# Hybrid attention block with 16384 experts on one core: gate products in two fp32r passes, second rows by ScalarE, choice stage of 19 expert groups

## The chip, the cores and the metric

One Trainium2 chip, of which the kernel uses one core. The metric is the device time of one execution in microseconds (us); lower is better.

## What is computed

One layer on 512 tokens of width 2048, float32. First attention of 16 heads with a projection in and out, then an expert layer: each of 8 heads chooses 16 of 16384 experts per token by two halves of 128 keys each (product keys), and the tokens' outputs are the chosen experts' values, weighted.

```python
def peer_ffn(xn, w_pq, sub_keys, u, v):
    ...
    s = jnp.einsum('thcd,hcnd->thcn', q, sub_keys, preferred_element_type=jnp.float32)
    s1, i1 = lax.top_k(s[:, :, 0], PEER_TOPK)
    s2, i2 = lax.top_k(s[:, :, 1], PEER_TOPK)
    ...
    top_s, pos = lax.top_k(cand, PEER_TOPK)
    idx = jnp.take_along_axis(cidx, pos, axis=-1)
    g = jax.nn.softmax(top_s, axis=-1).astype(xn.dtype)
    ...
        ub = u[ib]
        h = jax.nn.gelu(jnp.einsum('ted,td->te', ub, xb), approximate=False)
        vb = v[ib]
        return jnp.einsum('te,ted->td', gb * h, vb)
```

## The kernel before

It is written engine by engine: each engine's queue is a list in the order of the code, and semaphores tie the lists together. PE is TensorE (matmuls), DVE is VectorE, ACT is ScalarE, POOL is GpSimd, SP is SyncE with the queue that issues most DMAs.

Weights stream through in units of 1 MB. For each unit `load` (SyncE) brings it to `raw`, `split_hi` (ScalarE, L399) writes its high half `wh` in fp32r, `lo` (VectorE, L1128) the rest `wl`, and PE multiplies three times (high by high, high by low, low by high; L419 to L421 in `gemm`, L444 to L446 in `chunk_unit`). Two buffers of each: the hi of unit k+1 waits for PE's end of unit k-1.

The expert layer is dense for 336 of the 512 tokens: for all 128 blocks of 128 experts it computes gelu of tokens times `u`, multiplies by a table of gates (zero for what was not chosen), and multiplies by `v`. Another 128 tokens, and a strip of 48 (32 and 16, the "pair" rows) for `u` alone, are done by gathers of single rows: a "dot" (L1494 for the strip, L1596) multiplies a gathered row of `u`, and L1617 adds a gathered row of `v`.

The experts are in 32 groups of 4 blocks. The first `LAG` = 17 groups have their `u` units in the **choice stage** (68 units, counted k = 0 to 67, each one gemm of 16 x 3 matmuls of 336 columns), in which VectorE also finishes the choice and the gates are built. Then 15 **main groups** of 4 `u` and 4 `v` units each, then the **tail**: the `v` units of the 17 groups, two groups to a set of 8 units.

The gates are built in 96 batches of 4 tokens, two batches to a unit, from unit `GATE_FROM` = 16 to 63. For a token, 128 slots (head, rank) are on the partitions. The product of two 128x128 matrices, one holding a one at the slot's second key (`gh`, by L1456), the other holding the slot's weight at its first key (`hot_gate`, by L1469), gives the token's table of gates. Before, this is an fp32 matmul (L1970); on PE it stands inside the unit's gemm, behind the 6th and the 12th of 16 steps. ScalarE copies it out two batches at a time, one unit later (L1063), and every 8 batches a piece of 2 MB goes to `gate_scratch`; the next piece's first copy waits for that store.

The order on VectorE in unit k: lo(k+1), rows of the first batch of unit k+1 (`hot(ahead)`), a lookup or a pair dot where the tables `LOOK_AT` and `DOT_UNITS` say so, rows of the second batch. On ScalarE: gelu of unit k-1 (L1029), hi(k+1), the two copies, and in every second unit the weight rows of the next unit's first batch in VectorE's place (`rows_act`, L1038 and L1043). These wait only for the gate product that frees the buffer:

```python
                act.wait_ge(minus_done, b // 32 + 1)
                act.wait_ge(gate_done, b + 1)
```

`lookup` (L1433 to L1440) turns a rank into a key index by three operations; `take_slots` copies the turned slots of 128 tokens; `turn_pair` (PE) and `take_pair` replace the weights of the 48 tokens once their dots are done. After the stage SyncE issues, in this order, the acts and the gates of group 0 (L668, L672) and the weights of the second main unit; VectorE's `gate_mult` (L1584) waits for the former ahead of its lo for the latter.

Of the kernel before, what the change touches and what calls it, by code (L numbers as in the profile page):

```python
# [35 lines left out]
P = 128  # L36
# [14 lines left out]
LAG = 17  # L51
# [10 lines left out]
GATE_FROM = 16  # L62
# [4 lines left out]
LOOK_AT = {1: GATE_FROM, 3: GATE_FROM + 38}  # L67
# [5 lines left out]
ACT_ROWS = [_b for _b in range(0, (TD - PT - PB) // 4, 2 * GATE_STEP)]  # L73
# [3 lines left out]
DOT_UNITS = sorted([8, 9, 11, 12, 13, 14, 15] + list(range(20, 39)) + list(range(21, 38, 3)) +  # L77
                   list(range(40, 52)) + list(range(42, 52, 3)))
assert len(DOT_UNITS) == PN + NB and DOT_UNITS[PN - 1] == 38 and DOT_UNITS[PN] == 40
assert GATE_FROM == 16 and UT % 16 == 0 and FULL == UT // GT and PAIR_TURN < GATE_FROM + (SLOTS - PB - PT) // 4 + 32  # L80
# [59 lines left out]
def build(nc, x, attn_g, w_f, w_in, b_forget, q_g, k_g, w_out, ffn_g, ffn_row, w_pq, sub_keys, u, v, u_rows,  # L140
          v_rows, out):
    ctx = ExitStack()
    with ctx:
# [99 lines left out]
        look = gl[:, 0:1024]  # L243

        minus_g = at(7040, P)
        gate_piece = at(0, NKEYS * GT)
        h_out = [at(9616 + D, UT), at(9616 + D + UT, UT)]
        hot_gate = [at(8592, 512), at(8592 + 512, 512)]
# [90 lines left out]
        minus_done = sem("minus_done")  # L339
        diff_step = sem("diff_step")  # L340
# [483 lines left out]
        def _(act):  # L824
# [206 lines left out]
            def rows_act(b):  # L1031

                mine = slotT[b // 32 % 2]
                act.wait_ge(minus_done, b // 32 + 1)
                act.wait_ge(gate_done, b + 1)
                for n in range(4 * (b % 32), 4 * (b % 32) + 4):
                    dst = hot_gate[b % 2][:, n % 4 * P:n % 4 * P + P]
                    nc.scalar.activation(dst, iota128[:], ACT.Abs, bias=mine[:, 0, n:n + 1],  # L1038
                                         scale=-1.0).then_inc(diff_step, 1)
                for n in range(4 * (b % 32), 4 * (b % 32) + 4):  # L1040
                    dst = hot_gate[b % 2][:, n % 4 * P:n % 4 * P + P]
                    act.wait_ge(diff_step, 4 * ACT_ROWS.index(b) + n % 4 + 1)
                    last = nc.scalar.activation(dst, dst, ACT.Relu, bias=mine[:, 2, n:n + 1],  # L1043
                                                scale=minus_g[:, n:n + 1])
                last.then_inc(row_done, 1)

            for k in range(N_PROUNITS):
# [75 lines left out]
        def _(dve):  # L1123
# [327 lines left out]
            def hot(b):  # L1451
# [635 lines left out]
```

## Time and profile before

| | us |
|---|---|
| median of 3 runs | 3251.55 (3249.18 to 3255.22) |
| the profiled execution | 3252.24 |
| its span in the trace | 3250.5 |
| PE busy | 3216.1 |
| VectorE busy | 2263.4 |
| ScalarE busy | 1119.1 |
| GpSimd busy | 933.6 |

The trace begins at the first instruction; what lies around the span is 1.7 us. Matmuls are pipelined: a matmul's recorded length is longer than its slot, so the cost of one is read from start to start. The same holds in a lesser degree on VectorE and ScalarE, where an instruction begins before the recorded end of the one before.

### The profile page before, as it was taken

To read this page: it belongs to the slowest core of one execution; us is meant where nothing else is said; L and a number is where in the kernel's file an instruction comes from. 1 tells how busy PE (TensorE), PEld (TensorE's weight loads), DVE (VectorE), ACT (ScalarE), POOL (GpSimd) and SP (SyncE) were. 2 spreads that over 40 slices of the span, in tenths; PEclk is the share of its full clock that TensorE was granted. 3 is DMA by queue.
4 is the path that set the end of the run, shared out by engine and by line. 5 is a ranking of instruction groups with operands and counts; after the bars stand their busy time and mean duration, and the time that the engine had idled before them with its cause. 6 is when DMAs were issued, how large, how long until landed. Compare 5 with 4: busy or idle time off the path is not lost. (4 is left out here: it accounts for less than half of the span.)

```text
span 3250.5 us, 41510 instructions
## 1 busy us (share of the span) xinstructions
PE 3216.1 (99%) x16730; PEld 2818.6 (87%) x16730; DVE 2263.4 (70%) x2636; ACT 1119.1 (34%) x1172; POOL 933.6 (29%) x424
## 2 busy tenths in 40 slices
PE   8999999999999999999999999999999999999999
PEld 6878778887878899999999899889989988888887
DVE  5666541113027888887874888888889888888887
ACT  5232323334232233655553223223222322222221
POOL 4333333333434321111101323223322321223222
PEclk9999999999999999999999999999999999999999
DMA  3222222223233247889877989999989998888888
GB/s 144 78 78 90 77 78 78 78 78 141 92 116 121 88 161 255 304 316 318 311 243 265 352 333 352 336 341 345 358 332 335 350 343 312 320 336 340 343 319 317
DMA packets 171364, 777.87 MB, mean 239 GB/s; under 512 B 14064, under 2 KB 80752, under 8 KB 86384
## 3 DMA queue, kind: packets, MB, share of 16 engines
q1 hardware_dynamic: 127488, 457.77, 38.6%
q0 software_dynamic: 43776, 318.79, 26.3%
q8 instruction: 60, 0.98, 0.1%
q14 instruction: 40, 0.33, 0.0%
HBM read 731.10 MB, written 44.34 MB: 239 GB/s over the span
## 5 line engine op out<-in xcount | busy, mean ns | idle before, releaser
L419 PE MATMUL bank<-xh,wh 128*128 128x336 f32 (+1 forms) x3184 | 1105.8, 347 | 1.6 <-DVE wl L1128 1.6
L421 PE MATMUL bank<-xh,wl 128*128 128x336 f32 (+1 forms) x3184 | 1090.1, 342 | 0.0
L420 PE MATMUL bank<-xl,wh 128*128 128x336 f32 (+1 forms) x3184 | 1088.2, 342 | 0.0
L399 ACT ACTIVATE wh<-raw 128x2048 fp32r<-128x2048 f32 x344 | 658.0, 1913 | 999.0 <-PE bank L446 723.3
L1128 DVE TENSOR_TENSOR wl<-raw,wh 128x2048 fp32r<-128x2048 f32 x252 | 576.8, 2289 | 215.2 <-ACT wh L399 214.9
L419 PEld LDWEIGHTS bank<-xh,wh 128*128 128x128 f32 x3184 | 599.3, 188 | 46.5 <-issue 3.8
L420 PEld LDWEIGHTS bank<-xl,wh 128*128 128x128 f32 x3184 | 599.5, 188 | 44.7 <-issue 1.9
L421 PEld LDWEIGHTS bank<-xh,wl 128*128 128x128 f32 x3184 | 598.2, 188 | 45.1
L405 POOL TENSOR_TENSOR wl<-raw,wh 128x2048 fp32r<-128x2048 f32 x92 | 424.9, 4618 | 739.5 <-ACT wh L399 739.5
L444 PE MATMUL bank<-wh,xh 128*128 128x512 f32 x1072 | 417.1, 389 | 0.8 <-DVE stat L1302 0.8
L446 PE MATMUL bank<-wh,xl 128*128 128x512 f32 x1072 | 417.0, 389 | 0.0
L445 PE MATMUL bank<-wl,xh 128*128 128x512 f32 x1072 | 417.0, 389 | 0.0
L811 POOL DMA_INDIRECT arena<-in_u_rows,g_idx x128 | 249.3, 1947 | 456.2 <-DVE acc L1617 224.5
L811 POOL DMA_INDIRECT arena<-in_v_rows,g_idx x128 | 179.2, 1400 | 605.3 <-DVE acc L1617 317.3
L1596 DVE CUSTOM_DVE_ANT_0 arena<-arena 128x2048 f32<-128x2048 f32 x128 | 291.9, 2288 | 54.9 <-DMA arena<-in_u_rows,g_idx 54.8
L1617 DVE SCALAR_TENSOR_TENSOR acc<-arena,acc 128x2048 f32<-128x2048 f32 x128 | 300.5, 2347 | 3.5 <-DMA arena<-in_v_rows,g_idx 0.2
L444 PE MATMUL bank<-wh,gh 128*128 128x512 f32 x720 | 280.6, 390 | 1.6 <-DVE wl L1128 1.6
L446 PE MATMUL bank<-wh,gl 128*128 128x512 f32 x720 | 280.3, 389 | 0.0
L445 PE MATMUL bank<-wl,gh 128*128 128x512 f32 x720 | 280.2, 389 | 0.0
L444 PEld LDWEIGHTS bank<-wh,xh 128*128 128x128 f32 x1072 | 201.2, 188 | 42.8 <-DVE stat L1302 1.0
L445 PEld LDWEIGHTS bank<-wl,xh 128*128 128x128 f32 x1072 | 201.2, 188 | 41.8
L446 PEld LDWEIGHTS bank<-wh,xl 128*128 128x128 f32 x1072 | 201.2, 188 | 41.6
(211 smaller groups left out, 2803.3 us busy)
## 6 DMA issues: line engine op xcount, KB each, us to landing
raw<-in_u SPq DMA_DIRECT2D x128, 1024.0 KB, 5.8
raw<-in_v SPq DMA_DIRECT2D x128, 1024.0 KB, 6.2
raw<-in_w_in SPq DMA_DIRECT2D x56, 1024.0 KB, 4.8
gate_scratch<-arena SPq DMA_DIRECT2D x12, 2048.0 KB
arena<-gate_scratch SPq DMA_DIRECT2D x32, 768.0 KB, 9.0
raw<-in_w_out SPq DMA_DIRECT2D x16, 1024.0 KB, 4.9
raw<-in_w_pq SPq DMA_DIRECT2D x16, 1024.0 KB, 4.9
act_scratch<-arena SPq DMA_DIRECT2D x68, 168.0 KB, 4.4
```

The costliest lines, as they stand in the source:

```text
L399: nc.scalar.activation(wh[s][:], raw[s][:], ACT.Copy).then_inc(hi_done, 1)
L405: nc.gpsimd.tensor_tensor(wl[s][:], raw[s][:], wh[s][:].bitcast(F32), ALU.subtract).then_inc(lo_done, 1)
L419: nc.tensor.matmul(dst, w_h[:, c], xh[:, c, 0:width], start=(c == 0), stop=False)
L420: nc.tensor.matmul(dst, w_h[:, c], xl[:, c, 0:width], start=False, stop=False)
L421: last = nc.tensor.matmul(dst, w_l[:, c], xh[:, c, 0:width], start=False, stop=(c == KC - 1))
L444: nc.tensor.matmul(bank[:], a_hi(e)[:, rows_], w_h[:, e], start=begin, stop=False)
L445: nc.tensor.matmul(bank[:], a_hi(e)[:, rows_], w_l[:, e], start=False, stop=False)
L446: mm = nc.tensor.matmul(bank[:], a_lo(e)[:, rows_], w_h[:, e], start=False, stop=end)
L811: nc.gpsimd.indirect_dma_start(out=rows_g[n % ROW_BUFS], out_offset=None, in_=table, in_offset=bass.IndirectOffsetOnAxis(ap=g_idx[:, slot: ...
L1128: nc.vector.tensor_tensor(wl[k % 2][:], raw[k % 2][:], wh[k % 2][:].bitcast(F32), ALU.subtract).then_inc(lo_done, 1)
L1596: nc.vector.tensor_tensor_reduce(out=rows_g[b], in0=rows_g[b], in1=x_tok, scale=1.0, scalar=0.0, op0=ALU.mult, op1=ALU.add, accum_out=dots ...
L1617: nc.vector.scalar_tensor_tensor(out=acc[:, DB, :], in0=rows_g[b], scalar=dots[:, GM + j:GM + j + 1], in1=acc[:, DB, :], op0=ALU.mult, op1 ...
```

## The change

- The weight rows are written by VectorE for every batch, rounded to fp32r (`hot_hi`). The rest of a weight is not a separate row but a factor: `weight_rest` computes, per token and slot, rest divided by high weight, and ScalarE multiplies the high rows by this factor into `hot_lo` (4 instructions of 128x128 for each batch, one per-partition scale each).
- PE multiplies the keys by both, in fp32r, adding in PSUM: 8 matmuls of 128 columns for a batch where there were 4 in fp32. PE waits for `row_done` of every batch, ScalarE's rows for `hot_done` of every batch.
- `LAG` is 19: 76 units in the choice stage, 13 main groups, tail of 19 groups in 1 + 9 sets. Gates run from unit 25 to 72. Pair dots and lookups have other units; the pair turn stands one unit behind `pair_weights` (unit 65 and 64), where there were two (56 and 54).
- The lookup's scratch moves from `gl` to the arena, in float32.

```diff
-LAG = 17
+LAG = 19
...
-GATE_FROM = 16
+GATE_FROM = 25
 GATE_STEP = 2
 GATE_UNITS = DB * 32 // GATE_STEP
 GATE_PARTS = (2, 5)
 LOOK_ORDER = (2, 0, 1, 3)
-LOOK_AT = {1: GATE_FROM, 3: GATE_FROM + 38}
+LOOK_AT = {1: 14, 3: GATE_FROM + 38}
...
-ACT_ROWS = [_b for _b in range(0, (TD - PT - PB) // 4, 2 * GATE_STEP)]
...
-DOT_UNITS = sorted([8, 9, 11, 12, 13, 14, 15] + list(range(20, 39)) + list(range(21, 38, 3)) +
-                   list(range(40, 52)) + list(range(42, 52, 3)))
-assert len(DOT_UNITS) == PN + NB and DOT_UNITS[PN - 1] == 38 and DOT_UNITS[PN] == 40
-assert GATE_FROM == 16 and UT % 16 == 0 and FULL == UT // GT and PAIR_TURN < GATE_FROM + (SLOTS - PB - PT) // 4 + 32
+DOT_UNITS = sorted([8, 10, 12, 13, 14, 16, *range(18, 25), 18, 21, 24] +
+                   [_k for _k in range(25, 44) if _k not in (30, 36, 42)] +
+                   [_k for _k in range(45, 62) if _k != 52])
...
-        look = gl[:, 0:1024]
-
-        minus_g = at(7040, P)
+        look = at(8592, 1024)
+        rest_tmp = [at(8592 + P * n, P) for n in range(3)]
+
+        rest_of = [at(7040, P), ones[:]]
...
-        hot_gate = [at(8592, 512), at(8592 + 512, 512)]
+        hot_hi = [gl[:, 0:512], gl[:, 512:1024]]
+        hot_lo = [gl[:, 1024:1536], gh[:, 1024:1536]]
...
             def rows_act(b):
 
-                mine = slotT[b // 32 % 2]
-                act.wait_ge(minus_done, b // 32 + 1)
-                act.wait_ge(gate_done, b + 1)
-                for n in range(4 * (b % 32), 4 * (b % 32) + 4):
-                    dst = hot_gate[b % 2][:, n % 4 * P:n % 4 * P + P]
-                    nc.scalar.activation(dst, iota128[:], ACT.Abs, bias=mine[:, 0, n:n + 1],
-                                         scale=-1.0).then_inc(diff_step, 1)
-                for n in range(4 * (b % 32), 4 * (b % 32) + 4):
-                    dst = hot_gate[b % 2][:, n % 4 * P:n % 4 * P + P]
-                    act.wait_ge(diff_step, 4 * ACT_ROWS.index(b) + n % 4 + 1)
-                    last = nc.scalar.activation(dst, dst, ACT.Relu, bias=mine[:, 2, n:n + 1],
-                                                scale=minus_g[:, n:n + 1])
+                act.wait_ge(hot_done, b + 1)
+                for n in range(4):
+                    piece = slice(n * P, n * P + P)
+                    token = 4 * (b % 32) + n
+                    last = nc.scalar.activation(hot_lo[b % 2][:, piece], hot_hi[b % 2][:, piece].bitcast(F32), ACT.Copy,
+                                                scale=rest_of[b // 32 % 2][:, token:token + 1])
                 last.then_inc(row_done, 1)
...
+                ahead = GATE_STEP * (k + 1 - GATE_FROM)
+                if 0 <= ahead < DB * 32:
+                    rows_act(ahead)
                 if GATE_FROM < k <= GATE_FROM + GATE_UNITS:
                     for b in range(GATE_STEP * (k - 1 - GATE_FROM), GATE_STEP * (k - GATE_FROM)):
...
-                if GATE_STEP * (k + 1 - GATE_FROM) in ACT_ROWS:
-                    rows_act(GATE_STEP * (k + 1 - GATE_FROM))
+                if 0 <= ahead < DB * 32:
+                    rows_act(ahead + 1)
...
-                if n0 == 0:
-                    t = b // 32
-                    if t:
-                        dve.wait_ge(row_done, len([a for a in ACT_ROWS if a < b]))
-                    nc.vector.tensor_scalar(minus_g, turned_slots[:, 2, :], -1.0, None,
-                                            ALU.mult).then_inc(minus_done, 1)
-                if b in ACT_ROWS:
-                    dve.wait_ge(minus_done, b // 32 + 1)
-                for n in range(n0, n0 + 4) if b not in ACT_ROWS else ():
-                    last = nc.vector.tensor_scalar(hot_gate[b % 2][:, (n - n0) * P:(n - n0 + 1) * P], iota128[:],
+                for n in range(n0, n0 + 4):
+                    last = nc.vector.tensor_scalar(hot_hi[b % 2][:, (n - n0) * P:(n - n0 + 1) * P], iota128[:],
                                                    turned_slots[:, 0, n:n + 1], turned_slots[:, 2, n:n + 1],
                                                    ALU.is_equal, ALU.mult)
-                    if b % 4 == 0 and n == n0:
-                        last.then_inc(row_done, 1)
                 last.then_inc(hot_done, 1)
+
+            rests = [0]
+
+            def rested(ins):
+
+                rests[0] += 1
+                ins.then_inc(rest_step, 1)
+                dve.wait_ge(rest_step, rests[0])
+
+            def weight_rest(t, tokens=slice(0, P)):
+
+                w = slotT[t % 2][:, 2, tokens]
+                high, small, rest = (b[:, tokens] for b in rest_tmp)
+                rested(nc.vector.tensor_copy(high.bitcast(F32R), w))
+                nc.vector.tensor_tensor(rest, w, high, ALU.subtract)
+                rested(nc.vector.tensor_scalar(small, high, 0.0, None, ALU.is_equal))
+                rested(nc.vector.tensor_tensor(small, small, high, ALU.add))
+                rested(nc.vector.reciprocal(small, small))
+                rested(nc.vector.tensor_scalar(small, small, LARGE, -LARGE, ALU.min, ALU.max))
+                rested(nc.vector.tensor_tensor(rest_of[t % 2][:, tokens], rest, small, ALU.mult))
...
+                if LOOK_AT[1] <= k < LOOK_AT[1] + 4:
+                    lookup(1, (k - LOOK_AT[1]) // 2, (k - LOOK_AT[1]) % 2)
...
+                    weight_rest(0)
...
-                pe.wait_ge(hot_done, i * (4 * GATE_STEP) + b + 1)
-                if b % 4 == 0:
-                    pe.wait_ge(row_done, i * GATE_STEP + b // 4 + 1)
+                pe.wait_ge(row_done, i * (4 * GATE_STEP) + b + 1)
                 pe.wait_ge(gate_out, i * (4 * GATE_STEP) + b + 1)
                 for n in range(4):
-                    mm = nc.tensor.matmul(GATE_BANKS[b % 4][:, n * P:(n + 1) * P],
-                                          gh[:, (b % 2) * 512 + n * P:(b % 2) * 512 + (n + 1) * P].bitcast(F32),
-                                          hot_gate[b % 2][:, n * P:(n + 1) * P], start=True, stop=True)
+                    piece = slice(n * P, (n + 1) * P)
+                    keys = gh[:, (b % 2) * 512 + n * P:(b % 2) * 512 + (n + 1) * P]
+                    nc.tensor.matmul(GATE_BANKS[b % 4][:, piece], keys, hot_hi[b % 2][:, piece], start=True, stop=False)
+                    mm = nc.tensor.matmul(GATE_BANKS[b % 4][:, piece], keys, hot_lo[b % 2][:, piece], start=False,
+                                          stop=True)
                 mm.then_inc(gate_done, 1)
```

Where the wait stands is seen on ScalarE. Its queue over two units of the stage, before (L1029 gelu, L399 hi, L1063 copies, L1038 and L1043 rows):

```order
L1029 ACTIVATE arena<-bank 128x336 [waits h_stored0,unit_done]
L399 ACTIVATE wh<-raw 128x2048 [waits unit_done,raw_loaded1]
L1063 ACTIVATE arena<-bank 128x4x128 [waits gate_done] x2
L1038 ACTIVATE arena<-iota,arena 128x128 [waits gate_done,minus_done]
L1038 ACTIVATE arena<-iota,arena 128x128 x3
L1043 ACTIVATE arena<-arena 128x128 [waits diff_step] x4
L1029 ACTIVATE arena<-bank 128x336 [waits h_stored1,unit_done]
L399 ACTIVATE wh<-raw 128x2048 [waits unit_done,raw_loaded0]
```

And in the changed kernel (L1031 gelu, L401 hi, L1062 copies, L1039 second rows), one unit and the start of the next:

```order
L1031 ACTIVATE arena<-bank 128x336 [waits h_stored0,unit_done]
L401 ACTIVATE wh<-raw 128x2048 [waits unit_done,raw_loaded1]
L1039 ACTIVATE gl<-gl,ones 128x128 [waits hot_done]
L1039 ACTIVATE gl<-gl,ones 128x128 x3
L1062 ACTIVATE arena<-bank 128x4x128 [waits gate_done] x2
L1039 ACTIVATE gh<-gl,ones 128x128 [waits hot_done]
L1039 ACTIVATE gh<-gl,ones 128x128 x3
L1031 ACTIVATE arena<-bank 128x336 [waits h_stored1,unit_done]
L401 ACTIVATE wh<-raw 128x2048 [waits unit_done,raw_loaded0]
```

The rows now wait for `hot_done`, a semaphore of VectorE, twice in each unit, and the second wait stands ahead of the next gelu and hi. VectorE's queue for the same stretch of the changed kernel (L1127 lo, L1455 and L1460 hot rows, L1503 pair dot):

```order
L1127 TENSOR_TENSOR wl<-raw,wh 128x2048 [waits hi_done]
L1455 TENSOR_TENSOR gh<-iota,arena 128x512 [waits gate_done]
L1460 TENSOR_SCALAR gl<-iota,arena 128x128 x4
L1503 ISA acc,arena<-acc 128x2048 [waits pair_gathered0]
L1503 ISA arena 128x1
L1455 TENSOR_TENSOR gh<-iota,arena 128x512 [waits gate_done]
L1460 TENSOR_SCALAR gl<-iota,arena 128x128 x4
L1127 TENSOR_TENSOR wl<-raw,wh 128x2048 [waits hi_done]
```

The lo waits for ScalarE's hi and stands ahead of both batches' hot rows, as it did before; new is that every batch has its four L1460 rows.

## Rows read from the trace of the kernel before

**Rows 1.** The page: busy time, share of the span and instructions of each engine.
```profile
PE 3216.1 (99%) x16730; PEld 2818.6 (87%) x16730; DVE 2263.4 (70%) x2636; ACT 1119.1 (34%) x1172; POOL 933.6 (29%) x424
```

**Rows 2.** Windows: length, PE, PEld, DVE, ACT, POOL busy, granted clock, DMA share, GB/s.
```profile
1273.70:1726.55 452.85, 445.29 (x3079) 443.84 (x3078) 367.00 (x561) 255.44 (x360) 52.89 (x40) 0.99 0.82 284
...
1763.00:2673.00 910.00, 906.79 (x4912) 824.27 (x4911) 791.54 (x474) 266.72 (x207) 280.89 (x169) 1.00 0.91 342
...
2680.00:3240.00 560.00, 560.00 (x2473) 463.68 (x2472) 466.59 (x275) 155.93 (x93) 143.81 (x83) 1.00 0.87 330
```

**Rows 3.** Waits of PE: us in total, times, longest.
```profile
PE bank L1970 <- ACT arena L1043: 7.6, 4, 3.4
...
PE bank L419 <- DVE wl L1128: 1.6, 1, 1.6
```

**Rows 4.** Timeline of PE at a gate batch: start us, length us, instructions.
```profile
1505.61 0.32 PE L421 MATMUL bank<-xh,wl 128*128 128x336 f32 x1
1505.76 1.05 PE L1970 MATMUL bank<-arena,gh 128*128 128x128 f32 x8
1506.57 0.40 PE L419 MATMUL bank<-xh,wh 128*128 128x336 f32 x1
1506.80 0.32 PE L420 MATMUL bank<-xl,wh 128*128 128x336 f32 x1
```

**Rows 5.** Timeline of VectorE, one unit with a pair dot.
```profile
1454.33 2.28 DVE L1494 CUSTOM_DVE_ANT_0 acc<-acc 128x2048 f32<-128x2048 f32 x1
...
1456.54 0.68 DVE L1456 TENSOR_TENSOR gh<-iota,arena 128x512 fp32r<-128x512 f32 x1
1457.15 1.11 DVE L1469 TENSOR_SCALAR arena<-iota,arena 128x128 f32<-128x128 f32 x4
1458.18 2.28 DVE L1128 TENSOR_TENSOR wl<-raw,wh 128x2048 fp32r<-128x2048 f32 x1
1460.38 0.68 DVE L1456 TENSOR_TENSOR gh<-iota,arena 128x512 fp32r<-128x512 f32 x1
```

**Rows 6.** Timeline of ScalarE, the same unit.
```profile
1453.68 0.45 ACT L1029 ACTIVATE arena<-bank 128x336 f32<-128x336 f32 x1 [2.94 <-PE bank L421]
1454.02 1.92 ACT L399 ACTIVATE wh<-raw 128x2048 fp32r<-128x2048 f32 x1
1455.83 2.02 ACT L1063 ACTIVATE arena<-bank 128x512 f32<-128x512 f32 x2
1457.61 1.26 ACT L1038 ACTIVATE arena<-iota,arena 128x128 f32<-128x128 f32 x4
1458.75 1.66 ACT L1043 ACTIVATE arena<-arena 128x128 f32<-128x128 f32 x4
1462.84 0.45 ACT L1029 ACTIVATE arena<-bank 128x336 f32<-128x336 f32 x1 [2.43 <-PE bank L421]
```

**Rows 7.** Groups by line and form from 1300 to 2000 us: busy us, mean ns.
```profile
L1433 DVE TENSOR_TENSOR gl<-arena,iota 128x1024 fp32r<-128x1024 f32 x6 | 7.3, 1216 | 0.0
```

**Rows 8.** Timeline of PE, fp32r matmuls of 256 columns.
```profile
579.91 0.28 PE L1864 MATMUL bank<-gh,gl 128*128 128x256 f32 x1
580.03 0.28 PE L1864 MATMUL bank<-gl 128*128 128x256 f32 x1
```

**Rows 9.** Waits from 1200 to 2000 us: us in total, times, longest.
```profile
ACT arena L1063 <- DMA gate_scratch<-arena: 41.5, 11, 8.4
```

**Rows 10.** Timeline before the main groups: SyncE's queue, then ScalarE.
```profile
1742.70 0.55 SPq L672 DMA_DIRECT2D arena<-gate_scratch  x1
1746.65 0.33 SPq L391 DMA_DIRECT2D raw<-in_u  x1
...
1760.51 1.92 ACT L399 ACTIVATE wh<-raw 128x2048 fp32r<-128x2048 f32 x1 [4.01 <-DMA raw<-in_u]
```

**Rows 11.** Timeline of PE after its wait for the second rows.
```profile
1408.57 1.91 PE L1970 MATMUL bank<-arena,gh 128*128 128x128 f32 x8 [3.00 <-ACT arena L1043]
```

More of the change, by code:

```diff
@@ L72 @@
 PN = SLOTS // PQ
-ACT_ROWS = [_b for _b in range(0, (TD - PT - PB) // 4, 2 * GATE_STEP)]
+LARGE = 1.0e34
 assert GATE_STEP == 2
@@ L76 @@
 NB = SLOTS // QB
-DOT_UNITS = sorted([8, 9, 11, 12, 13, 14, 15] + list(range(20, 39)) + list(range(21, 38, 3)) +
-                   list(range(40, 52)) + list(range(42, 52, 3)))
-assert len(DOT_UNITS) == PN + NB and DOT_UNITS[PN - 1] == 38 and DOT_UNITS[PN] == 40
-assert GATE_FROM == 16 and UT % 16 == 0 and FULL == UT // GT and PAIR_TURN < GATE_FROM + (SLOTS - PB - PT) // 4 + 32
+DOT_UNITS = sorted([8, 10, 12, 13, 14, 16, *range(18, 25), 18, 21, 24] +
+                   [_k for _k in range(25, 44) if _k not in (30, 36, 42)] +
+                   [_k for _k in range(45, 62) if _k != 52])
+assert len(DOT_UNITS) == PN + NB and DOT_UNITS[PN - 1] == 43 and DOT_UNITS[PN] == 45
+assert UT % 16 == 0 and FULL == UT // GT and DOT_UNITS[-1] + 3 < PAIR_TURN <= GATE_FROM + 40
 EPS = 1e-6
@@ L338, in build @@
         hot_done = sem("hot_done")
-        minus_done = sem("minus_done")
-        diff_step = sem("diff_step")
+        rest_step = sem("rest_step")
         row_done = sem("row_done")
@@ L1436, in lookup @@
                 picked(nc.vector.tensor_tensor(
-                    look4, look4.bitcast(F32),
+                    look4, look4,
                     idx_f[:, t, 4 * half:4 * half + 4, c, :].unsqueeze(2).broadcast_to([P, PH // 2, TOPK, TOPK]),
                     ALU.mult))
-                nc.vector.tensor_reduce(slots[t][:, c, 64 * half:64 * half + 64], look3.bitcast(F32), AX.X,
+                nc.vector.tensor_reduce(slots[t][:, c, 64 * half:64 * half + 64], look3, AX.X,
                                         ALU.add).then_inc(slots_done, 1)
@@ L1550, in _ @@
                     hot(ahead)
-                for t in (1, DB):
-                    if LOOK_AT[t] <= k < LOOK_AT[t] + 4:
-                        lookup(t, (k - LOOK_AT[t]) // 2, (k - LOOK_AT[t]) % 2)
+                if LOOK_AT[DB] <= k < LOOK_AT[DB] + 4:
+                    lookup(DB, (k - LOOK_AT[DB]) // 2, (k - LOOK_AT[DB]) % 2)
                 for j, at_unit in enumerate(DOT_UNITS):
@@ L1556, in _ @@
                         pair_dot(j)
-                if k == 20:
+                if k == GATE_FROM + 4:
                     dve.wait_ge(side_chosen, 16 * QB)
@@ L1566, in _ @@
                         take_slots(t)
+                        weight_rest(t)
                 if k == PAIR_TURN:
                     take_pair()
+                    weight_rest(DB - 1, slice(P - PT - PB, P))
                 if k == LOOK_AT[DB] + 4:
```

## The prediction

> **What bounds the kernel now.** I read the page's totals first, then busy times by stage, then who waited for whom, then the timeline of one unit on three engines. The totals say that PE is occupied for nearly the whole span and VectorE for 70% of it [rows 1]. By stage this holds everywhere: in the choice stage (units 16 to 63, the 452.85 us from 1273.70 on) PE is busy 445.29 us, in the main groups 906.79 of 910 us, in the tail sets all of 560 us [rows 2]. PE's waits for its gate rows come to 7.6 us in all [rows 3]. So before the change the time is PE's work, and the other engines are covered.
>
> The timeline of one unit gives the sizes. A gemm matmul of 336 columns takes a slot of 0.15 us; a gate batch, begun at 1505.76, pushes the second gemm matmul behind it to 1506.80, so it costs 1.04 - 0.15 = 0.89 us [rows 4]. From one gelu to the next is 9.16 us (1453.68 to 1462.84) [rows 6]: 7.38 us of gemm and two batches.
>
> VectorE [rows 5], from start to start: a pair dot 2.21 us, the rows of one batch (the L1456 row and four L1469 rows) 1.64 us, the low half of the weights ("lo") 2.20 us. ScalarE [rows 6]: gelu 0.34, high half of the weights ("hi") 1.81 to the next start and 1.92 to its end, the two gate evacuations 1.78, four row instructions of L1038 1.14.
>
> **The change, part by part.** *(1) The new wait makes a ring.* What ScalarE did in every fourth batch (L1038, L1043) waited for nothing newer than an old gate product. Now every batch's second rows on ScalarE wait for `hot_done`, and behind them in ScalarE's in-order queue stand the gelu and the hi of the next unit. VectorE's lo of that unit waits for this hi, and its next hot rows stand behind that lo. Followed once round, from hi(k+1) to hi(k+2): hi 1.92, lo 2.20, hot rows of the first batch 1.64, pair dot 2.21, hot rows of the second batch to their end 1.71 (0.60, then the 1.11 of four pieces), second rows 1.14, gelu 0.34. Sum 11.16 us. No PE work is in this ring: the gate products that the hot rows wait for are of the unit before and ready. A unit can't be shorter than its longest loop, and PE's own, 9.16 us, is shorter. So I expect PE to turn from bound to waiting, about 2 us in each unit.
>
> In a unit without a pair dot ScalarE's own row of work is longer than VectorE's: hi 1.92, lo 2.20, first hot rows 1.71, second rows 1.14, evacuations 1.78, second rows 1.14, gelu 0.34 = 10.23 us. In the four units with lookups (63 to 66) three more operations of about 1.22 us each [rows 7] stand where the dot stood: 11.16 - 2.21 + 3.66 = 12.61 us. The list of dots has 32 units in the new stage. Sum: 32 x 11.16 + 4 x 12.61 + 12 x 10.23 = 530.3 us against 452.85 us now: **+77 us**.
>
> The row instruction is the unknown in it. Before there are two forms of 128x128 on ScalarE: L1038 with one per-partition operand, 1.14 for four, and L1043 with two, from 1458.75 on with a recorded length of 1.66 against 1.26 [rows 6]. The new one has one such operand (the scale), so I take 1.14. At L1043's pace, 0.40 more for four, the stage would cost 32 x 0.40 + 12 x 0.80 = 22 us more. The Trainium skill, "ScalarE: Activation LUTs", section "What ACT_TABLE_LOAD costs", says that each such pointer operand adds about 93 ns; the trace agrees (0.40 for four), and by that rule too the sum stays at the lower end.
>
> *(2) The product in two fp32r passes.* PE issues 8 fp32r matmuls of 128 columns for a batch, where the profile now shows 8 passes for 4 fp32 matmuls. The narrowest full fp32r matmul is 256 columns at a spacing of 0.12 us (579.91 to 580.03) [rows 8]. Half of that for the columns alone gives 0.06, a batch of 0.48 us; if each fp32r matmul cost a whole fp32 one (0.89 / 4), 1.78 us. PE's unit is then between 8.3 and 10.9 us, all of it under 11.16. So I put this part at **0** in either direction: the ring covers it. Were the ring gone, the low end would be worth 96 x 0.41 = 39 us. The fp32r output of the rows on VectorE and the work that leaves ScalarE (L1038, L1043) cost nothing apart.
>
> *(3) Rests of the weights* (seven small operations at three places, and once more for 48 tokens). VectorE waits 1.14 + 0.34 + 1.92 = 3.4 us in each ring for ScalarE; seven operations at about 0.3 us fit. Cost 0; without that cover some 2 us each.
>
> *(4) Gates from unit 25, 19 groups.* Eight units move from the main loop into the stage, at the same matmuls: 0 on PE. Before unit 25 VectorE has lo, eight lookups and 16 dots: 17 x 2.20 + 8 x 3.66 + 16 x 2.21 = 102 us in 17 units of 7.38 = 125 us; covered. The turn of the pair's weights now stands one unit behind their making, where there were two: PE must wait for VectorE's unit 64, hot rows and lookup included. It may lose a lookup, a batch of rows and the copies, about 8 us, or nothing, since the ring catches up: **+4 us**.
>
> *(5) Gate pieces.* ScalarE's evacuation waits for the store of the piece before. It arrives 9.16 - 2.02 = 7.1 us after the last one, and over 11 pieces waits 41.5 us, 3.8 each [rows 9]: a store needs some 11 us, the longest 7.1 + 8.4 = 15.5. In the ring ScalarE comes back after 11.16 - 1.78 = 9.4 us and has 0.9 us to spare (the second hot rows end later). The mean store is 0.6 us beyond that, 7 us over eleven; the long ones weigh more, but traffic per us falls. **+8** (ends 0 and 20, half of today's waits).
>
> *(6) Start of the main groups.* Only three units lie between the last gates and the main loop, four before. The queue on SyncE issues the first main weights behind the acts and gates; they landed 13.9 us later (1746.65 to 1760.51), and PE lost 1.6 us [rows 3, 10]. PE arrives 7.4 us earlier now; the load, at best behind the gate load at 1742.70, is 3.6 us earlier. **+5 us** (0 to 7).
>
> Sum: 77 + 4 + 8 + 5 = +94 us, on the profiled execution's 3252.24 us. That stands 0.7 us above the median of the three runs. Forecast 3347 us (2.9% slower). The measurement of this kernel can tell about 0.2%, 6.5 us, from no change.
>
> **Rivals.** *Ring hidden, PE stays the bound* (ends on the other side). If the second rows were ready before the ring binds, that is if the whole ring took under PE's 9.16 us, the shorter passes would show. For it: ScalarE is busy 255 of 453 us in this stage [rows 2]. Against: idle time doesn't help a queue in order, and the seven terms are recorded lengths. Price: 0.48 us a batch saves 39 us and (6) takes 5: 3218 us. The Trainium skill, "TensorE: Matmul & The Clock Gate", section "Back-to-back issue gap", gives 81 ns for a 128-column matmul with its weight load; by that (an estimate) a batch is 0.65 us and the time 3234 us. No run here shows this form. Chance 0.05.
>
> *The passes are no cheaper and the ring is hidden*, so that the change does nothing for PE: 3252 + 5 = 3257 us. Chance 0.03.
>
> *The tail becomes the bound too.* 19 groups leave 51 slots to nine tail sets where 40 went to eight: six sets take 6 slots, three 5. VectorE in the tail is busy 466.6 of 560 us and DMA moves 330 GB/s at 0.87 [rows 2]; one slot more is two gathers of 1 MB and some 4.5 us of VectorE in a set of 62 us (eight of the 72 units that the 560 us hold), so 364 GB/s and 52 + 4.5 of 62 us. The main groups live with 342 GB/s at 0.91. If the queues gave no more than 355, a set would take 1.6 us more, 10 to 20 us in all. Time 3362 us. Chance 0.12.
>
> *The clock falls from 2.4 to 1.2 GHz in the ring's gaps.* After the 3.00 us wait at 1408.57 a batch has a recorded length of 1.91 instead of 1.05 us, and the stage's granted clock averages 0.99 [rows 2, 4, 11]. One percent of 453 us spread on the two longest waits (3.0 and 3.4 us [rows 3]) is about 2 us for each. One such fall in each unit makes PE's unit 11.2 us, just covered; two make it 13.2, +2 x 44 = 88 us more: 3435 us. PE's 2 us come split (for lo, for the rows), each shorter than 3 us. Chance 0.03.
>
> **How the numbers follow.** The forecast gets 0.77; the likeliest time is its own. The low end: parts (4) to (6) at nothing gives 3329, and the ring 0.3 us shorter in 48 units 3315. The high end: the slower row form (+22), stores (+11), pair turn and main start (+6), the tail (+15) give 3401. Range 3315 to 3400: it leaves out both hidden-ring rivals (0.08), the clock, and some of both ends. Faster 0.05, same 0.03, slower 0.92.
>
> **What would show it.** ScalarE's row instructions wait for VectorE's hot rows in nearly every unit; VectorE's lo waits for hi some 3 us in each; gelu to gelu is 11.2 us with a dot and 10.2 us without; the stage of 48 units is about 530 to 545 us; PE's busy share there falls under 90%. The longest single PE waits stand at unit 65 and at the first main units. If gelu to gelu is under 9.2 us, the ring is wrong; if PE shows no wait and yet units of 11 us, part (2) is. If the stage is right and the time isn't, the tail's waits decide.

## The result, and the profile after

The changed kernel takes 3404.28 us (median of 6 runs, 3394.0 to 3408.81) against 3252.14 us for the kernel before in the same runs: the ratio is 1.0461, interval 1.0443 to 1.048. The forecast was 3347 us. The direction and the first mechanism were right; the size was 57 us short, and the time is 4 us beyond the range. One of the runs told of below, a run of the last experiment, took 3940 us at a granted clock of 0.753 and is left out of that experiment's ratio.

| us | before | after |
|---|---|---|
| span of the profiled execution | 3250.5 | 3404.6 |
| PE busy | 3216.1 | 3260.3 |
| VectorE busy | 2263.4 | 2288.2 |
| ScalarE busy | 1119.1 | 1173.5 |
| mean granted clock of PE | 0.998 | 0.987 |

First the windows of the changed kernel, to be laid beside [rows 2]: the choice stage from its first gates, and the tail. Columns as there.

```profile
1339.20:1904.40 565.20, 474.98 (x3060) 459.05 (x3060) 363.04 (x638) 308.21 (x574) 36.22 (x32) 0.94 0.62 213
...
2730.00:3390.00 660.00, 634.28 (x2751) 522.27 (x2750) 547.87 (x324) 173.68 (x104) 180.42 (x106) 0.98 0.88 333
```

PE is busy 475 of 565 us in the stage where it was busy 445 of 453, and 634 of 660 us in the tail where it had no gap. So time is lost in two stages, not in one. The forecast's signs hold in part: PE's share in the stage is 84%, under the 90% named, but the stage takes 565 us, not 530 to 545, and the longest waits of PE stand at the first gates (8.7 us), the pair's turn (7.9) and in the tail (up to 5.0), not at the first main units (1.8). The waits of PE in the whole span, beside [rows 3] (us in total, times, longest):

```profile
PE bank L1983 <- ACT arena L1062: 59.0, 36, 4.7
PE bank L446 <- DVE wl L1127: 27.8, 9, 5.0
...
PE bank L421 <- DVE wl L1127: 15.6, 21, 1.8
PE bank L1983 <- ACT gl L1039: 8.7, 1, 8.7
PE bank L1973 <- DVE arena L1518: 7.9, 1, 7.9
```

L1983 is the new gate product, L1062 the copy out of a gate bank, L446 the tail's and main loop's matmul, L1973 the turn of the pair's weights.

ScalarE's timeline over two units with a pair dot, beside [rows 6]. The first of them (to 1565.59) holds a wait for a gate store, the second does not:

```profile
1557.80 1.29 ACT L1039 ACTIVATE gl<-gl,ones 128x128 fp32r<-128x128 f32 x4 [3.99 <-DVE gl L1460]
1562.75 1.91 ACT L1062 ACTIVATE arena<-bank 128x512 f32<-128x512 f32 x2 [3.67 <-DMA gate_scratch<-arena]
1564.45 1.23 ACT L1039 ACTIVATE gh<-gl,ones 128x128 fp32r<-128x128 f32 x4
1565.59 0.43 ACT L1031 ACTIVATE arena<-bank 128x336 f32<-128x336 f32 x1
1565.92 1.90 ACT L401 ACTIVATE wh<-raw 128x2048 fp32r<-128x2048 f32 x1
1571.82 1.28 ACT L1039 ACTIVATE gl<-gl,ones 128x128 fp32r<-128x128 f32 x4 [3.99 <-DVE gl L1460]
1573.00 2.04 ACT L1062 ACTIVATE arena<-bank 128x512 f32<-128x512 f32 x2
1575.65 1.28 ACT L1039 ACTIVATE gh<-gl,ones 128x128 fp32r<-128x128 f32 x4 [0.61 <-DVE gl L1460]
1576.84 0.43 ACT L1031 ACTIVATE arena<-bank 128x336 f32<-128x336 f32 x1
```

From gelu to gelu (1565.59 to 1576.84) are 11.25 us. Between the hi at 1565.92 and the first second rows ScalarE waits 3.99 us for VectorE, and before the others 0.61 us more: this is the ring of the prediction. VectorE's side, some units earlier, beside [rows 5]:

```profile
1505.95 2.29 DVE L1127 TENSOR_TENSOR wl<-raw,wh 128x2048 fp32r<-128x2048 f32 x1 [0.46 <-ACT wh L401]
1508.16 0.68 DVE L1455 TENSOR_TENSOR gh<-iota,arena 128x512 fp32r<-128x512 f32 x1
1508.77 1.11 DVE L1460 TENSOR_SCALAR gl<-iota,arena 128x128 fp32r<-128x128 f32 x4
1509.79 2.29 DVE L1503 CUSTOM_DVE_ANT_0 acc<-acc 128x2048 f32<-128x2048 f32 x1
...
1512.00 0.69 DVE L1455 TENSOR_TENSOR gh<-iota,arena 128x512 fp32r<-128x512 f32 x1
1512.60 1.11 DVE L1460 TENSOR_SCALAR gl<-iota,arena 128x128 fp32r<-128x128 f32 x4
```

One lo, four hot rows, a dot, four hot rows, in the same lengths as before. The gate product on PE, beside [rows 4]:

```profile
1504.70 0.22 PE L1983 MATMUL bank<-gl,gh 128*128 128x128 f32 x1
1504.76 0.27 PE L1984 MATMUL bank<-gh 128*128 128x128 f32 x1
1504.87 0.28 PE L1983 MATMUL bank<-gl,gh 128*128 128x128 f32 x1
1504.98 0.28 PE L1984 MATMUL bank<-gh 128*128 128x128 f32 x1
...
1505.54 0.37 PE L421 MATMUL bank<-xh,wh 128*128 128x336 f32 x1
1505.74 0.31 PE L422 MATMUL bank<-xl,wh 128*128 128x336 f32 x1
```

An fp32r matmul of 128 columns stands every 0.11 us (only the second follows the first after 0.06). From the batch's start (1504.70) to the second gemm matmul behind it (1505.74) are 1.04 us, less one slot of 0.15: 0.89 us, the very length of the fp32 product. The number of passes is the same too: the profile has 768 matmul records and 768 weight loads for the product, before as after.

Gelu to gelu by unit gives the account of the stage, over 49 intervals from the one that holds the first rows: 575.5 us against 460.5, +115. A unit with a dot takes 11.25 us, one without 10.26, one with a lookup 12.81. Eight intervals, each with a wait of ScalarE for a gate store, take 13.5 to 14.2 us, together 23.6 us more than their kind (two of the eight have no dot). A ninth of 13.95 us has no such wait: there VectorE turns the pair's weights, 1.14 us more in the ring than in its neighbours. The first interval takes 20.25 us. It begins so (VectorE, then ScalarE):

```profile
1345.35 2.29 DVE L1503 CUSTOM_DVE_ANT_0 acc<-acc 128x2048 f32<-128x2048 f32 x1 [3.94 <-DMA acc<-in_u_rows,arena]
...
1349.31 1.28 ACT L1039 ACTIVATE gl<-gl,arena 128x128 fp32r<-128x128 f32 x4 [15.19 <-DVE gl L1460]
```

The first second rows waited 15.19 us, since VectorE stood at dots of unit 24 whose gathers were late. The other 39 us of the 154 us of span come behind the stage. In each of six tail sets PE waits once, 26 us together, and each of these waits is followed by a stretch at the lower clock. One of them (VectorE, then PE, the last two lines from that stretch):

```profile
3001.97 2.35 DVE L1630 SCALAR_TENSOR_TENSOR acc<-arena,acc 128x2048 f32<-128x2048 f32 x1 [1.21 <-DMA arena<-in_v_rows,g_idx]
3007.17 2.29 DVE L1609 CUSTOM_DVE_ANT_0 arena<-arena 128x2048 f32<-128x2048 f32 x1 [2.85 <-DMA arena<-in_u_rows,g_idx]
...
3009.39 1.75 DVE L470 TENSOR_TENSOR acc<-bank,acc 128x1536 f32<-128x1536 f32 x1
3011.06 2.28 DVE L1127 TENSOR_TENSOR wl<-raw,wh 128x2048 fp32r<-128x2048 f32 x1
...
3013.39 0.50 PE L446 MATMUL bank<-wh,xh 128*128 128x512 f32 x1 [4.59 <-DVE wl L1127]
...
3015.76 0.63 PE L446 MATMUL bank<-wh,xh 128*128 128x512 f32 x1
3016.19 0.63 PE L447 MATMUL bank<-wl,xh 128*128 128x512 f32 x1
```

The dot at 3007.17 waited 2.85 us for its gather; behind it stand the adding of a chunk and the lo at 3011.06 that PE waits for. From about 3014 to 3017 a matmul of 512 columns starts every 0.43 us, at a granted clock of 0.54 to 0.61 (1.2 GHz in most of it), and every 0.23 us from 3017.60 on, at 1.00: nine slow ones are 1.8 us lost on top of the wait. In the kernel before VectorE waited for `u` gathers four times in the tail, 3.7 us in all; here it waits ten times, 21.4 us.

### The profile page after: what moved, and what is told of

Read it like the earlier page. It is cut to its first block, busy times and chain, and to the rows that moved or that the text cites. A ratio compares the mean times of both kernels' runs of the same rounds, so it can differ in the third digit from the quotient of the medians.

```text
span 3404.6 us, 41678 instructions
## 1 busy us (share of the span) xinstructions
PE 3260.3 (96%) x16730; PEld 2843.6 (84%) x16730; DVE 2288.2 (67%) x2740; ACT 1173.5 (34%) x1387; POOL 938.4 (28%) x424
## 4 chain that ended last, share of the span: by engine, by line
PE 70%; DVE 12%; DMA 9%; ACT 7%; issue 2%; POOL 1%; SPq 0%; ACTq 0%; DVEq 0%
PE bank L421 12%; PE bank L423 12%; PE bank L422 12%; PE bank L446 10%; PE bank L448 10%; PE bank L447 10%; DVE wl L1127 4%; ACT wh L401 3%; DMA gate_scratch<-arena 3%; DMA arena<-in_u_rows,g_idx 3%; DVE gl L1460 2%; DVE acc L1503 2%; DMA acc<-in_u_rows,arena 1%; DVE gh L1455 1%; ACT gh L1039 1%
## 5 line engine op out<-in xcount | busy, mean ns | idle before, releaser
L401 ACT ACTIVATE wh<-raw 128x2048 fp32r<-128x2048 f32 x344 | 657.6, 1912 | 1010.7 <-PE bank L448 744.0
L1127 DVE TENSOR_TENSOR wl<-raw,wh 128x2048 fp32r<-128x2048 f32 x252 | 577.0, 2290 | 342.7 <-ACT wh L401 342.3
L421 PEld LDWEIGHTS bank<-xh,wh 128*128 128x128 f32 x3184 | 605.5, 190 | 66.2 <-issue 15.4
L446 PE MATMUL bank<-wh,xh 128*128 128x512 f32 x1168 | 459.1, 393 | 26.5 <-DVE wl L1127 25.7
L448 PE MATMUL bank<-wh,xl 128*128 128x512 f32 x1168 | 458.1, 392 | 0.0
L447 PE MATMUL bank<-wl,xh 128*128 128x512 f32 x1168 | 458.0, 392 | 0.0
L813 POOL DMA_INDIRECT arena<-in_v_rows,g_idx x128 | 203.4, 1589 | 612.1 <-DVE acc L1630 318.0
L813 POOL DMA_INDIRECT arena<-in_u_rows,g_idx x128 | 225.2, 1760 | 423.0 <-DVE arena L1609 222.8
L446 PEld LDWEIGHTS bank<-wh,xh 128*128 128x128 f32 x1168 | 221.5, 190 | 75.5 <-DVE wl L1127 28.3
L447 PEld LDWEIGHTS bank<-wl,xh 128*128 128x128 f32 x1168 | 221.6, 190 | 46.2
L446 PE MATMUL bank<-wh,gh 128*128 128x512 f32 x624 | 243.3, 390 | 2.1 <-DVE wl L1127 2.1
L448 PE MATMUL bank<-wh,gl 128*128 128x512 f32 x624 | 242.9, 389 | 0.0
L447 PE MATMUL bank<-wl,gh 128*128 128x512 f32 x624 | 242.8, 389 | 0.0
```

Source lines behind the costliest of these rows:

```text
L401: nc.scalar.activation(wh[s][:], raw[s][:], ACT.Copy).then_inc(hi_done, 1)
L421: nc.tensor.matmul(dst, w_h[:, c], xh[:, c, 0:width], start=(c == 0), stop=False)
L446: nc.tensor.matmul(bank[:], a_hi(e)[:, rows_], w_h[:, e], start=begin, stop=False)
L447: nc.tensor.matmul(bank[:], a_hi(e)[:, rows_], w_l[:, e], start=False, stop=False)
L448: mm = nc.tensor.matmul(bank[:], a_lo(e)[:, rows_], w_h[:, e], start=False, stop=end)
L813: nc.gpsimd.indirect_dma_start(out=rows_g[n % ROW_BUFS], out_offset=None, in_=table, in_offset=bass.IndirectOffsetOnAxis(ap=g_idx[:, slot: ...
```

## The experiments

What holds for all: L numbers of the rows are those of the experiment's own code. Medians stand with the ratio to the kernel before in the same runs and its interval.

### Second rows behind hi

```diff
-                if 0 <= ahead < DB * 32:
-                    rows_act(ahead)
+                if 0 <= ahead - GATE_STEP < DB * 32:
+                    rows_act(ahead - GATE_STEP + 1)
...
                 if 0 <= ahead < DB * 32:
-                    rows_act(ahead + 1)
+                    rows_act(ahead)
```

> The changed kernel with one move in ScalarE's order: the second rows of a unit's second batch stand behind the next unit's hi, no longer ahead of its gelu and hi. Same instructions. Ring theory: what is left of the ring (hi 1.92, lo 2.20, first hot rows 1.71, second rows 1.14, gelu 0.34 = 7.3 us) is under PE's 9.16 us, a unit takes 9.2 us, and of the 154 us that the change cost the 115 us of the choice stage go: 3289 us, 3277 us if the waits for the gate store go too. What stays is the tail. Rival: PE waits most for the copies of the gate banks (59 us in all), so the copies are the bound: then the order of rows and hi matters little, above 3390 us.

Measured: 3286.89 us, ratio 1.0111 (1.0094 to 1.0128). The instructions are the same, 117 us are gone. ScalarE's timeline over one unit (L1031 gelu, L401 hi, L1039 second rows, L1062 copies):

```profile
1564.02 0.45 ACT L1031 ACTIVATE arena<-bank 128x336 f32<-128x336 f32 x1 [1.62 <-PE bank L423]
1564.37 1.91 ACT L401 ACTIVATE wh<-raw 128x2048 fp32r<-128x2048 f32 x1
1566.17 1.27 ACT L1039 ACTIVATE gh<-gl,ones 128x128 fp32r<-128x128 f32 x4
1567.34 2.07 ACT L1062 ACTIVATE arena<-bank 128x512 f32<-128x512 f32 x2
1570.27 1.28 ACT L1039 ACTIVATE gl<-gl,ones 128x128 fp32r<-128x128 f32 x4 [0.86 <-DVE gl L1460]
1573.17 0.45 ACT L1031 ACTIVATE arena<-bank 128x336 f32<-128x336 f32 x1 [1.61 <-PE bank L423]
```

Gelu to gelu is 9.15 us and ScalarE again waits for PE (1.6 us ahead of the gelu). PE's waits for copies, 59 us in the changed kernel, are not among its waits here: they were the form in which PE spent the ring's idle time, not a cause.

### 19 groups alone

```diff
-LAG = 17
+LAG = 19
```

(on the kernel before)

> The kernel before with 19 groups in the choice stage in place of 17 and nothing else. Tail theory (51 slots on nine sets, six sets of six): PE waits some 4 us in each of six tail sets and runs at the lower clock behind each wait, together 38 us: 3290 us. Rival: the tail's waits come from what the new gates leave behind, not from the slots: 3252 us, within 5.

Measured: 3291.98 us, 1.0125 (1.0108 to 1.0142), 42 us over the kernel before in the same runs. The waits of PE in the tail (2700 to 3200 us) are like those of the changed kernel, six of them:

```profile
PE bank L444 <- DVE wl L1128: 26.4, 6, 5.0
```

So the tail's 38 us belong to the number of groups, whatever makes the gates. The mean granted clock from 2730 to 3240 us is 0.97 here.

### Copies ahead of both rows

```diff
                 ahead = GATE_STEP * (k + 1 - GATE_FROM)
-                if 0 <= ahead < DB * 32:
-                    rows_act(ahead)
                 if GATE_FROM < k <= GATE_FROM + GATE_UNITS:
...
                 if 0 <= ahead < DB * 32:
+                    rows_act(ahead)
                     rows_act(ahead + 1)
```

> The changed kernel with the two copies of the gate banks ahead of both second rows on ScalarE. The ring through the pair dot stays (11.25 us a unit). Theory that the gate store is in the ring: copies and their wait for the store now lie beside lo and hot rows with some 4.8 us to spare, so the eleven units of 14.0 us fall to 11.25 (31 us) and the units without a dot from 10.27 to 9.2 (12 us): 3361 us. Rival: the store's traffic, not its place, makes these units long: 3395 to 3404 us.

Measured: 3366.15 us, 1.0351 (1.0332 to 1.037), 38 us less than the changed kernel. One unit of ScalarE (L1060 copies):

```profile
1574.25 0.43 ACT L1031 ACTIVATE arena<-bank 128x336 f32<-128x336 f32 x1
...
1576.38 2.01 ACT L1060 ACTIVATE arena<-bank 128x512 f32<-128x512 f32 x2
1580.47 1.28 ACT L1039 ACTIVATE gl<-gl,ones 128x128 fp32r<-128x128 f32 x4 [2.08 <-DVE gl L1459]
1584.31 1.28 ACT L1039 ACTIVATE gh<-gl,ones 128x128 fp32r<-128x128 f32 x4 [2.56 <-DVE gl L1459]
1585.50 0.43 ACT L1031 ACTIVATE arena<-bank 128x336 f32<-128x336 f32 x1
```

The unit with a dot stays at 11.25 us to the hundredth (1574.25 to 1585.50), since copies and first rows were not in its ring. Units without a dot fall to 9.03 to 9.04 us, and no interval with a store and a dot stands out any more (11.64 us at most). The store carries the same bytes, but not only its place changed: it also lands sooner, after 8.0 to 8.4 us, where in the changed kernel eight stores took 12.7 to 13.2. Those eight were all issued 0.7 us behind a gather of a pair row (GpSimd, then SyncE, changed kernel):

```profile
1548.99 1.15 POOL L799 DMA_INDIRECT acc<-in_u_rows,arena  x1 [10.11 <-DVE arena L1503]
...
1549.74 0.39 SPq L664 DMA_DIRECT2D gate_scratch<-arena  x1
```

The four stores there without a gather took 8.1 to 8.3 us, and ScalarE did not wait for them. With the copies first the store is issued some 4.4 us ahead of the gather. So the store term goes with the order of the queue, but this run moves two things, the place of the wait and the length of the store, and does not tell their shares. The first interval fell as well, from 20.25 to 14.51 us; it differs from run to run.

### First tail dot behind lo

```diff
                 for j in before[2:]:
                     add_row(s - 1, j)
-                dot(s, 0)
                 tail_chunk(q, 0)
                 tail_lo(q, 3)
+                dot(s, 0)
```

> The changed kernel with one move in VectorE's tail: in each set the first dot stands behind the lo of the fourth weight unit, no longer ahead of it. Theory: PE waits for this lo, which stands behind a dot that waits for its gather (2.9 us) and takes 2.2 us; without it the six waits of 3.7 to 5.0 us and the clock behind them go: 3366 us. Rival: VectorE or the gathers are full in these sets, and the wait comes back at a later lo: 3395 to 3404 us.

Measured: 3366.81 us, 1.0361 (1.0343 to 1.0378), 37 us less. Of the 27.8 us of waits at L446 there are left:

```profile
PE bank L446 <- DVE wl L1127: 2.3, 4, 1.1
```

VectorE and the gathers were not full: the wait was one of order. The sets take 65 us again, as before the change, with the DMA at up to 0.95 and 373 GB/s.

### Both moves

The changed kernel with the second rows behind hi and the first tail dot behind lo.

> The changed kernel with both moves: second rows of the second batch behind hi, first dot of a tail set behind lo. Theory that ring and tail are two causes that add up: 3287 less 37 us, 3250 us, level with the kernel before (within 6 us), since eight fp32r matmuls of 128 columns fill 0.89 us just as the fp32 product does. Rival: a third cause behind the two (DMA in 19 groups, VectorE): 3265 us and more. Rival on the other side: the new product is cheaper once PE sets the pace: 3240 us or less.

Measured: 3256.67 us, 1.0016 (1.0002 to 1.0029). Together the moves take back 148 us (117 and 37 alone), so ring and tail, with what hangs on them, account for all but 5 us of the change. The profiled execution was one of the slower ones (3266.03 us of 3248 to 3270). What is left in it of PE's waits beyond those of before is mainly the entry to the gates:

```profile
PE bank L1983 <- ACT gl L1039: 7.3, 1, 7.3
```

Next come 5.5 us at L446, none longer than 2.1. The rival of a cheaper product is out: with PE setting the pace a unit takes 9.15 us, as before.

### New gates at 17 groups

`LAG`, `GATE_FROM`, `LOOK_AT` and `DOT_UNITS` as in the kernel before, the new gate products, second rows behind hi.

> The new gate products with the second rows behind hi, in the kernel before's plan: 17 groups, gates from unit 16, its units for dots and lookups. Theory: PE sets the pace in every stage, at the same 9.17 us a unit; of the 13 us that the stage lost before to waits for second rows and to the clock some 5 to 10 go: 3240 to 3252 us. Rival: units with two dots leave VectorE no room beside four rows more in each fourth batch (2.20 + 3.28 + 4.42 = 9.9 us): 3255 to 3270 us.

Measured: 3253.66 us, 1.0009 (1.0 to 1.0018). That is neither the gain that I expected (3240 to 3252 us) nor the rival's loss. The waits for second rows came to 8.3 us in place of 7.6, so my 5 to 10 us did not come: the form of the product alone is worth nothing either way.

### More rows in the ring

```diff
                 last.then_inc(row_done, 1)
+                for n in range(4) if b % 2 else ():
+                    piece = slice(n * P, n * P + P)
+                    nc.scalar.activation(banks[2][:, piece], hot_hi[1][:, piece].bitcast(F32), ACT.Copy,
+                                         scale=rest_of[b // 32 % 2][:, 0:1])
```

> The changed kernel with four more row instructions of ScalarE (128x128, into an unused PSUM bank) behind the second rows of each unit's second batch; nothing waits for them. Ring theory: they stand in the ring, 1.14 us and more in each of 47 units: 54 us or more on 3404, 3455 to 3465 us. Rival: ScalarE, busy about half of the stage, takes them in its idle time: 3404 us.

Measured: 3446.03 us, 1.0599 (1.0583 to 1.0615), +42 us, which is 9 us under the range expected. The second rows, the added ones, the gelu of one unit:

```profile
1585.62 1.28 ACT L1039 ACTIVATE gh<-gl,ones 128x128 fp32r<-128x128 f32 x4 [0.67 <-DVE gl L1464]
1586.81 1.23 ACT L1044 ACTIVATE bank<-gl,ones 128x128 f32<-128x128 f32 x4
1587.98 0.43 ACT L1031 ACTIVATE arena<-bank 128x336 f32<-128x336 f32 x1
```

The added four take 1.17 us from start to the gelu's start, and units with a dot take 12.42 us in place of 11.25: exactly that. It is less than 54 us in sum because the eight intervals with a store take 13.2 to 14.4 us, about as before (the added time counts against the wait for the store), and the first interval was 4.9 us shorter.

### One pass

```diff
-                pe.wait_ge(row_done, i * (4 * GATE_STEP) + b + 1)
+                pe.wait_ge(hot_done, i * (4 * GATE_STEP) + b + 1)
...
-                    nc.tensor.matmul(GATE_BANKS[b % 4][:, piece], keys, hot_hi[b % 2][:, piece], start=True, stop=False)
-                    mm = nc.tensor.matmul(GATE_BANKS[b % 4][:, piece], keys, hot_lo[b % 2][:, piece], start=False,
-                                          stop=True)
+                    mm = nc.tensor.matmul(GATE_BANKS[b % 4][:, piece], keys, hot_hi[b % 2][:, piece], start=True,
+                                          stop=True)
```

and no second rows on ScalarE, at 17 groups.

> The new gates in the kernel before's plan (17 groups, gates from unit 16) with the second rows and the second pass left out: the gates carry weights rounded to fp32r. ScalarE writes no rows, so there is no ring. Theory that a matmul of 128 columns costs 0.11 us whatever the form: four in place of eight save 0.44 us in each of 96 batches, 42 us, with VectorE's full units giving some back: 3208 to 3225 us. Rival: VectorE bounds the units with two dots (9.9 us against PE's 8.3): 3225 to 3250 us.

Measured: 3234.56 us, 0.9945 (0.9931 to 0.9959). That is 17 us gained and not 42, within the rival's range: PE waited 15.4 us, in 13 waits, for VectorE's hot rows, which the rival named as the cause, and besides 6.8 us for the copies and 6.1 us for a lo.

### The entry's dots moved

On top of both moves:

```diff
-DOT_UNITS = sorted([8, 10, 12, 13, 14, 16, *range(18, 25), 18, 21, 24] +
+DOT_UNITS = sorted([8, 10, 12, 13, 14, 15, 16, 17, *range(18, 24), 18, 21] +
```

> Second rows behind hi and first tail dot behind lo, as measured at 3257 us, and also the two dots of unit 24 moved to units 15 and 17. Theory: PE's 7.3 us wait at the first gate batch comes from dots of unit 24 that wait for their gathers ahead of the first hot rows on VectorE; without them 5 to 8 us go: 3249 us. Rival: gathers are late by traffic (two queues full in units 18 to 24), so the wait stays wherever the dots stand: 3255 to 3258 us.

Measured: 3254.73 us, 1.0008 (0.9998 to 1.0017). The wait at the first gates is gone, but PE's waits for a lo have grown from 4.4 to 7.0 us, the longest of them 4.9 us, some four units ahead of the gates (the gelu intervals there are 8.2 and 14.1 us where 7.4 was usual); in front of that lo a pair dot waited 4.9 us for its gather. 2 us are within the spread of the two medians, so the rival fits better: the gathers come late where the dots stand now, too. The profiles can't be laid side by side for more than the places of the waits, since this one is of the fastest of 11 executions and that of both moves of the second slowest of 11. I have no run that thins the dots out.

### One pass at 19 groups

One pass and the entry's dots moved, as in the last two edits, at 19 groups and with the first tail dot behind lo.

> One pass (second rows and second pass left out, so that the gates carry weights rounded to fp32r) in the plan of 19 groups, with the first tail dot behind lo and the dots of unit 24 moved. No unit with gates has two dots here, so VectorE has 7.7 us of work in a unit of 8.3. Theory: the 42 us of four matmuls fewer in 96 batches come whole: 3208 us, 27 us under the same pass at 17 groups (3235), where VectorE was late with hot rows. Rival: the tail's fuller sets take it back: 3225 us and more.

Measured: 3219.11 us, 0.9892 (0.9874 to 0.991), the fastest version of the study, 33 us under the kernel before. A batch on PE:

```profile
1561.44 0.56 PE L1979 MATMUL bank<-gl,gh 128*128 128x128 f32 x4
1561.83 0.37 PE L421 MATMUL bank<-xh,wh 128*128 128x336 f32 x1
1562.04 0.31 PE L422 MATMUL bank<-xl,wh 128*128 128x336 f32 x1
```

From 1561.44 to 1562.04 less a slot of 0.15 is 0.45 us, half of 0.89, and units take 8.25 us. The 11 us missing to 3208 are in part in these waits, of which the first is the largest (then 3.8 us at the pair's turn, 3.1 for the tail's lo, 2.1 for copies):

```profile
PE bank L421 <- DVE wl L1123: 8.6, 4, 4.8
```

It is a trade, not a free gain: the gates lose what the second rows carried.

## Why the prediction was wrong in its size

The ring, the main cost, was right. What failed is the tail, which the sum put at 0 and the range at 15 us at most and which cost 38; next to it the gate stores (8 put, 24 measured) and the entry (not in the sum, 9). (The terms add up to 3346 us, not 3347; that changes nothing in this.)

**The ring** (77 us). Right, in place and size. The sum of seven recorded lengths gave 11.16 us, measured 11.25; without a dot 10.23, measured 10.26; with a lookup 12.61, measured 12.81. One move in ScalarE's queue takes it away, and 1.17 us put into it lengthen it by 1.17 us. The choice among the two forms of row instruction was right too: four take 1.14 to 1.19 us in the new form (1575.65 to 1576.84).

**Two fp32r passes** (0). Right while the ring holds. But the low end of the batch, 0.48 us, was no bound: a matmul of 128 columns takes 0.11 us, nearly as long as the 0.12 of one with 256 [rows 8]. So the rival in which PE gains 39 us was mispriced by all of it, as were the Trainium skill's 81 ns for such a matmul with its weight load ("TensorE: Matmul & The Clock Gate", "Back-to-back issue gap"): here it is 110 ns in fp32r, and the measurement decides. The weight loads follow each other at the same 0.11 us; whether they are what holds the product there, no run tells.

**The gate stores** (+8). Under-sized by 16 us: eight units were longer by 23.6 us together, and ScalarE's wait was 3.2 to 3.8 us in each. I expected the store to be faster with less traffic. It was not: from the end of the copies to the next ones, ScalarE came back after 9.4 us and waited 3.7 more, 13.1 us, against the 10.9 us on average before. That average was the wrong figure to go by: in the trace of 19 groups alone, whose gates are those of the kernel before, six of twelve stores land in 8.2 to 8.3 us and the others in 9.6 to 16.2. The changed kernel issued each of its first eight stores 0.7 us behind a gather, and these were the long ones; at 8.3 us they would have been hidden in the 9.4 us. The run with the copies first took this term away together with the ScalarE loop of units without a dot.

**The tail** (0, in the range up to 15, as a rival 10 to 20 at 0.12). This is the step that failed most: it cost 38 us, and 19 groups alone cost 42. I asked whether VectorE and DMA are full on average over a set, found 56.5 of 62 us, and took that as room. They were indeed not full, and the 355 GB/s at which I let the rival begin were passed without a wait once the dot stood elsewhere. I did not ask what the sixth slot puts ahead of a lo that PE waits for: a second add of a row, 2.3 us, between the third lo and the first dot. The dot stood in front of the fourth lo before as well, but now it waits 2.5 to 4.2 us for its gather in each of the six sets. And each wait of 3.7 to 5.0 us has the lower clock behind it: the six sets' windows have 0.97, some 2 us each, which the tail's price left out: 26 us of waits and 12 of clock. The length of a set in the rival, 62 us, was wrong as well: it is 65 us in the kernel before and 71 with such a wait.

**The pair's turn** (+4). PE waited 7.9 us there, as priced at the upper end, but in a ring a wait of PE is only another form of its idle time: the interval in which it falls took 13.95 us against the 12.81 of its neighbours, and the 1.14 us more are VectorE's own turning, which stands in the ring. So +1.

**The start of the main groups** (+5). PE waited 1.8 us against 1.6, but behind the wait it ran at a granted clock of 0.54 to 0.61 for 4 us, where the kernel before stayed at 1.00. So +2; why the loads were in time is open, no run was made on it.

**The rests of the weights** (0). Right: the seven operations take 2.6 us from 1502.90 on, and the two intervals that they touch (11.26 and 14.20 us) are those of their kind within 0.2.

**The entry** (0, not in the sum). 9 us in this execution; PE's wait at the first gates was 8.7 us here and 2.6 to 7.3 in other runs with the same dots. I checked VectorE's work before unit 25, 102 of 125 us, not the gathers of the two dots of unit 24 right ahead of the first hot rows.

**The clock's rival** (0.03). In the stage the granted clock fell to 0.94 on average, far more often than I allowed, and it cost next to nothing there: the units of 11.25 us stand at that number throughout, since the ring covers it. Behind the tail's waits, where PE sets the pace, it cost.

Sum by these: 94 + 4 (ring) + 16 (stores) + 38 (tail) + 9 (entry) - 3 (turn) - 3 (main start) = 155 us against the 154 measured.

## What to carry to other kernels

When a wait is added on an in-order queue, follow what stands behind it on that queue until the path closes on itself, and add the recorded lengths: the sum is the new shortest period, idle shares notwithstanding. A stage of which work is moved has to be read in the order of its queue too: ask what the additional instruction stands ahead of, not whether the engine has room on average. And before a product is split into more passes, look at the start-to-start time of a matmul of that width: below some width it stops falling (here 0.23, 0.15, 0.12 and 0.11 us for 512, 336, 256 and 128 columns in fp32r). And before the mean of a wait is used as a price, look at its single cases: the stores' 11 us were a mixture of 8 and up to 16.

## What the runs showed of the hardware that was not expected

- An fp32r matmul of 128x128 by 128 columns takes 0.11 us from start to start with its weight load, one by 256 columns 0.12 us: eight of the narrow ones are as long as four fp32 products of 128 columns (0.89 us both).
- A PE wait of some 4 us is followed by a stretch at 1.2 GHz (granted clock 0.97 over windows of 63 us, 1.00 in those without such a wait), which makes it cost about 2 us more than its own length where PE sets the pace: nine matmuls at 0.43 us in place of 0.23.
- The 2 MB store of gates took 12.7 to 13.2 us when it was issued 0.7 us behind a 1 MB gather of rows, and 8.1 to 8.3 us when no gather was under way (changed kernel, eight and four stores). The run with the tail dot moved has the same eight long ones (12.5 to 13.4) and four short ones (8.3 to 8.4); with the copies first, where the gather is issued behind the store, all twelve take 8.0 to 8.4. No run moved the gather alone, so that it is the cause is read from these cases and not from an experiment.
